# A 31-tap depthwise conv split between TensorE and VectorE: 24 taps stay as matmuls, 7 go to VectorE

## The reference

```
p = x @ w_in     # [B_a | C_a | v_a | val_b | gate_b | g_a | g_b], 1024 columns each
y_a = (B_a * conv3_causal(C_a * v_a)) @ w_out_a
u   = val_b * sigmoid(gate_b)
u   = conv31_causal(u) + conv_b_bias        # depthwise: each channel with its own 31 weights
y_b = silu(LayerNorm(u)) @ w_out_b
x1  = LayerNorm(alpha*x + (sigmoid(g_a)*y_a + sigmoid(g_b)*y_b) @ w_o)
x2  = LayerNorm(alpha*x1 + relu(x1 @ w_up)**2 @ w_down)
```

## Time and profile before

| | us |
|---|---|
| median of 3 runs (lowest, highest) | 2285.79 (2278.91, 2288.07) |
| the profiled execution | 2279.74 |
| its span, slowest core (fastest core) | 2278.2 (2259.3) |
| PE busy | 2159.3, 95% |
| ACT busy | 903.1, 40% |
| DVE busy | 865.2, 38% |
| POOL busy | 625.4, 27% |
| the 2048 conv matmuls, line 424 | 124.0 |

### The profile page before, as it was taken

The page is one execution under the profiler, slowest core; times in us unless marked ns, Lnnn a source line. Parts: engine busy times, 40 slices in busy tenths (PEclk is TensorE's granted clock), DMA queues, the critical chain, the costliest instruction groups (busy, mean ns, idle before and its releaser), DMA issues.

```text
span 2278.2 us, 33259 instructions; the slowest of 8 cores (2259.3 to 2278.2 us)
## 1 busy us (share of the span) xinstructions
PE 2159.3 (95%) x11568; PEld 961.8 (42%) x11568; DVE 865.2 (38%) x1199; ACT 903.1 (40%) x1422; POOL 625.4 (27%) x524
## 2 busy tenths in 40 slices
PE   6997699999997999999999999999999999999896
PEld 2443244443443444444444444444444444444342
DVE  2211154551346233651346034803381237323604
ACT  1111132354324633454335533462346334642562
POOL 1000022330426042421433043404350426030321
PEclk9998899999998999999999999999999999999998
DMA  9999759599886778655566447555665556445452
GB/s 153 140 136 132 187 162 195 188 187 198 207 204 177 200 161 260 198 176 159 190 200 183 156 175 217 180 171 176 188 187 175 177 167 212 140 148 175 139 185 74
DMA packets 107828, 400.69 MB, mean 176 GB/s; under 512 B 13712, under 2 KB 54928, under 8 KB 68752
## 3 DMA queue, kind: packets, MB, share of 16 engines
q1 hardware_dynamic: 84672, 306.21, 42.8%
q0 software_dynamic: 12624, 73.47, 20.7%
q10 hardware_dynamic: 10368, 18.88, 2.6%
HBM read 425.78 MB, written 58.79 MB: 213 GB/s over the span
## 4 chain that ended last, share of the span: by engine, by line
PE 73%; DVE 8%; DMA 7%; SPq 7%; issue 2%; POOL 1%; ACT 1%; DVEq 0%; ACTq 0%; POOLq 0%
PE ps L272 68%; SPq L101 7%; PE ps L424 4%; DVE sgt L295 3%; DMA yblk<-tt 1%; DMA wbf<-wsl 1%; DMA wsl<-wbf 1%; DMA h<-wblk 1%; DVE cvb L282 1%; DMA wsl<-wblk 1%; DMA xft<-xblk 1%; DVE sumS L282 1%; DVE cvh L300 1%; POOL sumQ L282 1%; POOL tt L282 1%
## 5 line engine op out<-in xcount | busy, mean ns | idle before, releaser
L272 PE MATMUL ps<-xbf,wsl 128*128 128x512 bf16 x2624 | 599.1, 381 | 10.8 <-DVE apre L282 6.0
L272 PE MATMUL ps<-bx,wsl 128*128 128x512 bf16 x2560 | 571.0, 380 | 7.6 <-ACT bx L278 7.3
L272 PE MATMUL ps<-h,wsl 128*128 128x512 bf16 x2496 | 545.6, 380 | 9.8 <-DMA wsl<-wblk 9.6
L278 ACT ACTIVATE tA<-ps 128x512 f32<-128x512 f32 x448 | 264.7, 594 | 436.8 <-PE ps L272 403.1
L272 PEld LDWEIGHTS ps<-xbf,wsl 128*128 128x128 bf16 x2624 | 253.2, 98 | 327.3 <-issue 33.5
L272 PEld LDWEIGHTS ps<-bx,wsl 128*128 128x128 bf16 x2560 | 249.2, 98 | 316.4 <-issue 21.7
L272 PEld LDWEIGHTS ps<-h,wsl 128*128 128x128 bf16 x2496 | 244.6, 98 | 307.0 <-issue 14.9
L282 POOL TENSOR_TENSOR tt<-tt,rstd 128x512 f32<-128x512 f32 x178 | 243.5, 1368 | 99.3 <-ACT rstd L278 76.9
L272 PE MATMUL ps<-xbf,h 128*128 128x512 bf16 x1024 | 233.8, 391 | 38.3 <-DVE cvb L295 18.9
L282 POOL TENSOR_TENSOR tt<-res,mu 128x512 f32<-128x512 f32 x112 | 158.4, 1414 | 389.0 <-DMA yblk<-tt 203.5
L282 POOL TENSOR_TENSOR tt<-u,mu 128x512 f32<-128x512 f32 x66 | 90.1, 1366 | 593.7 <-ACT mu L278 539.8
(11 more groups left out here) (66 smaller groups left out, 1150.4 us busy)
## 6 DMA issues: line engine op xcount, KB each, us to landing
wsl<-wbf SPq DMA_DIRECT2D x240, 1024.0 KB, 6.0
rep<-u0d SPq DMA_DIRECT2D x256, 135.0 KB, 3.9
wbf<-wblk POOLq DMA_DIRECT2D x24, 1024.0 KB, 23.7
wsl<-wblk POOLq DMA_DIRECT2D x16, 1024.0 KB, 15.3
yblk<-tt ACTq DMA_DIRECT2D x56, 256.0 KB, 6.0
xbf<-xblk POOLq DMA_DIRECT2D x13, 1024.0 KB, 13.8
xft<-xblk POOLq DMA_DIRECT2D x32, 256.0 KB, 6.5
wbf<-wsl SPq DMA_DIRECT2D x8, 1024.0 KB, 19.5
```

The costliest lines, as they stand in the source:

```text
L272: last = e.matmul(bank_ap, lhsT=l, rhs=r, start=(start and idx == 0), stop=(stop and idx == n - 1))
L278: S.op("act", lambda e: e.activation(out=out, in_=in_, func=func, bias=bias, scale=scale), reads=reads, writes=writes)
```

## The change

KS goes from 8 to 6: TensorE keeps the youngest 24 taps, in 24 matmuls for each conv. The oldest KD = 7 taps go to DVE. A new tile `un` (three buffers, 128 channels x 518 tokens, bf16) is filled from `u0d` by one further DMA in `spread`, without the spreading over partitions. In `conv` ACT writes `u` with the bias as before; then the new `conv_taps` adds tap after tap to `u` with `stt`, in place; only then ACT squares `u` (no longer the bank), `spread` for j + 3 is issued, and the sums are taken. The places move: behind j = 1, 3, 5 of S3 the conv with four taps, with three taps, the Square and the rest behind j = 2, 4, 6; none in S1A(i+1); five in up, behind f = 2, 8, 14, 20, 26. The eight convs of pass 0 keep their places, with all seven taps. The conv weights are halved on chip, as before, the seven in a tile `cwn` of their own.

```diff
-KS = 8
+KS = 6
+KD = KB - 4 * KS
+NUN = 3
+NW = T + KD - 1
...
         def spread(i, j):
...
-            c0 = i * T + 1
+            c0 = i * T + 1 + 32 - 4 * KS
...
+            r = (8 * i + j) % NUN
+            c0 = i * T + HL + 1 - KB
+            S.dma("sp", unsem[r], un[r][:], u0d[j, :, c0:c0 + NW],
+                  reads=[("u0d", i % 2, j)] + ([("u0dh", j)] if i == 0 else []), writes=[("un", r)])
...
-        def conv(i, j, st_):
+        def conv(i, j, st_, whole=True):
...
             act(u[:, j, :], ps[b][:, :], AF.Identity, reads=[("ps", b), "cst"], writes=[("u", j)],
                 bias=pv[:, 0, j:j + 1])
+            rel(b)
+            conv_taps(i, j, st_, 0, KD if whole else KD - 3)
+
+        def conv_taps(i, j, st_, lo, hi):
+            r = (8 * i + j) % NUN
+            for k in range(lo, hi):
+                stt(u[:, j, :], un[r][:, k:k + T], cwn[:, j, k:k + 1], u[:, j, :], ALU.mult, ALU.add,
+                    reads=[("un", r), ("u", j), "cwn"], writes=[("u", j)])
+            if hi < KD:
+                return
             q = rt("sq", 2)
-            act(sq[q][:], ps[b][:, :], AF.Square, reads=[("ps", b), "cst"], writes=[("sq", q)],
-                bias=pv[:, 0, j:j + 1])
-            rel(b)
+            act(sq[q][:], u[:, j, :], AF.Square, reads=[("u", j)], writes=[("sq", q)])
             if j + NREP < 8:
                 spread(i, j + NREP)
...
                 if not last and j in (1, 3, 5):
-                    conv(i + 1, j // 2, stC)
+                    conv(i + 1, j // 2, stC, False)
+                if not last and j in (2, 4, 6):
+                    conv_taps(i + 1, j // 2 - 1, stC, KD - 3, KD)
...
-                    if j in (2, 5):
-                        conv(i + 1, 3 + j // 4, stC)
...
-                if not last and f in (8, 16, 24):
-                    conv(i + 1, 4 + f // 8, stC)
+                if not last and f % 6 == 2 and f < 30:
+                    conv(i + 1, 3 + f // 6, stC)
```

More of the change, by code:

```diff
@@ L132, in build_nc @@
     ident4_d = nc.dram_tensor("ident4", [128, 32], F32, kind="ExternalInput").ap()
+    cwn_d = nc.dram_tensor("cwn", [128, 8, KD], F32, kind="ExternalInput").ap()
     cwa_d = nc.dram_tensor("cwa", [128, 8, KA], F32, kind="ExternalInput").ap()
@@ L164, in build_nc @@
         wsl = [sb(f"wsl{i}", [128, 4096], BF16) for i in range(NS)]
+        cwn = sb("cwn_s", [128, 8, KD], F32)
+        un = [sb(f"un{i}", [128, NW], BF16) for i in range(NUN)]
         cwa = sb("cwa_s", [128, 8, KA], F32)
@@ L186, in build_nc @@
         osem = [S.new_sem(f"o{i}") for i in range(NTT)]
-        csem = [S.new_sem(f"k{i}") for i in range(5)]
+        csem = [S.new_sem(f"k{i}") for i in range(6)]
+        unsem = [S.new_sem(f"un{i}") for i in range(NUN)]
         repsem = [S.new_sem(f"rp{i}") for i in range(NREP)]
@@ L697, in build_nc @@
         S.dma("sp", csem[2], pv[:], pv_d, writes=["cst"])
+        S.dma("sp", csem[5], cwn[:], cwn_d, writes=["cwn"])
+        tsc("dve", cwn[:], cwn[:], 0.5, None, ALU.mult, None, reads=["cwn"], writes=["cwn"])
         for j in range(8):
@@ L901 @@
     wblk = _weight_blocks(f(w_in), f(w_out_a), f(w_out_b), f(w_o), f(w_up), f(w_down))
-    taps = np.zeros((4 * KS, D), np.float32)
-    taps[4 * KS - KB:] = f(conv_b_w)
+    taps = f(conv_b_w)[KB - 4 * KS:]
+    cwn = np.ascontiguousarray(f(conv_b_w)[:KB - 4 * KS].T.reshape(8, 128, KD).transpose(1, 0, 2))
     cwb = np.ascontiguousarray(
@@ L919 @@
             xh = np.ascontiguousarray(x[b, t0 - HL:t0, :].reshape(HL, 8, 128).transpose(2, 1, 0))
-        in_maps.append({"xblk": xb, "xh": xh, "wblk": wblk, "cwb": cwb, "cwa": cwa, "pv": pv,
+        in_maps.append({"xblk": xb, "xh": xh, "wblk": wblk, "cwb": cwb, "cwn": cwn, "cwa": cwa, "pv": pv,
                         "ident4": np.tile(np.eye(32, dtype=np.float32), (4, 1))})
```

## The result

The changed kernel takes **1.0578 times the time of the one before, 95% interval 1.0525 to 1.0631** (both run side by side). Its profiled execution took 2413.4 us against 2279.7: **+133.6 us, where the prediction had +76**. The sign is as forecast; the time lies above the upper end of the range, 2405.

What follows compares the result with a forecast made beforehand. TensorE, busy 95%, bounds the kernel; after the change ACT ends last in up. Passes 1 to 6 +59.4, pass 0 +3.5, start +13: +76 on 2279.7, 2356 profiled, 2362 by the median; range 2322 to 2405.

Steps and rivals of the forecast that it cites:

- The hold of ACT per conv: Up stage: one conv holds ACT 7.34 us, from Identity through seven DVE taps (0.85 us step) to the Square's end.
- The count of the up stage: Up's start to the end of down's first block: 83.6 us instead of 68.0, +15.6, as ACT ends last.
- S1A: Stage losing both its convs: 3.7 us less, plus half of a 1.09 us wait kept, -4.3 us a pass.
- Rivals (1): Up's stall is covered by eight banks, all 29.6 us come off: 2250, by the median 2256; chance 0.04.
- (2): Taps step by 0.60 us, ACT's hold is 5.84: +8, 2288, by the median 2294; chance 0.06.
- (3): Taps step by 1.62 us everywhere, something other than POOL slowing them: +203, 2559, by the median 2565; chance 0.03.
- rival (4): Weights come late behind SP's waits, in each of seven passes: +35, 2391, by the median 2397; chance 0.09.
- The start: F and first S1A: +16 us from DVE's late sums, less 2.8: +13 us, between 8 and 17.
- the -2.8 for shorter convs in F: Six convs stand in F, where TensorE gains 6 x 0.46 = 2.8 us.
- Pass 0: First pass: longer up stage covers down's waits for weights, 10.9 - 1.6 - 4.3 - 1.4 = +3.5 us.
- The step that failed: S3: splitting taps 4 and 3 delays a sigmoid about 3 us, covered by banks; put at nothing.
- 9.9 a pass: Passes 1 to 6: up +15.6, S1A -4.3, S3's three shorter convs -1.4, net +9.9 each, +59.4 together.

Runs made afterwards that it cites:

- both edits: Changed kernel with the convs' Square, spread and sums four f later in up and one j later in S3: 0.9955, again 0.9940, of the kernel before; profiled 2265.8 us.

## Why the prediction was right in sign and short in size

**Right, term by term.** The hold of ACT per conv was put at 7.34 us. The trace has 7.29, from the Identity at 1294.15 to the next operation at 1301.44 (ACT's timeline, and the taps on DVE's):

```profile
1294.15 0.67 ACT L285 ACTIVATE u<-ps,pv_s 128x512 f32<-128x512 f32 x1
1300.90 0.63 ACT L285 ACTIVATE sq<-u 128x512 f32<-128x512 f32 x1 [6.08 <-DVE u L302]
1301.44 0.58 ACT L285 ACTIVATE tA<-ps 128x512 f32<-128x512 f32 x1
```

```profile
1294.92 5.88 DVE L302 SCALAR_TENSOR_TENSOR u<-un,cwn_s,u 128x512 f32<-128x512 bf16 x7 [2.20 <-ACT u L285]
```

Seven taps took 5.88 us for 5.85, and the wait ahead of the Square is 6.08 us for all five convs of this pass. The count of the up stage gave 83.6 us to the end of down's first block, measured 82.9, with the waits where it had them: about 2.3 at f=22 (1.60), 1 to 3 at f=28 (2.49), and the rest at down's first block (5.71). S1A gave back 3.8 us for 4.3. Rivals (1), (2) and (3) are out by the same rows, and rival (4) with them, since waits for wsl<-wbf sum to 3.7 us in the span. (The +203 and +35 of rivals (3) and (4) count from the forecast's 2356, not from the kernel before.)

**The start**: forecast +13 (+16 less 2.8), measured +18.9 (S3(0) at 378.37, before 359.47 in the earlier trace rows). TensorE, start of S3(0), and the fourth block of down in pass 0 (for the next paragraph):

```profile
378.37 3.57 PE L279 MATMUL ps<-apre,wsl 128*128 128x512 bf16 x8 [4.12 <-DVE apre L289]
...
598.10 36.52 PE L279 MATMUL ps<-h,wsl 128*128 128x512 bf16 x157 [5.77 <-DMA wsl<-wblk]
```

S1A to S3 took 304.01 to 378.37, 17.1 us more for a forecast of 16, the sums of j=0 and 1 at 35.7 us for a forecast of 36. What failed is the -2.8 for shorter convs in F: from the first conv to S1A TensorE gained 1.5 us (47.2 us, before 48.7), and the first conv itself, which waits for rep (27.1 us; 12.0 before), started at 256.85, 3.4 us later than before. In the changed kernel it starts between 252.6 and 260.5 us, depending on the core, before between 249.7 and 253.5. I did not test what sets it.

**Pass 0**: forecast +3.5, measured +3.9 (start of down's fourth block 598.10, before 575.31 in the earlier trace rows, less the start's 18.9). That the two agree is luck. The forecast put three blocks of down, 3 x 6.9 us, between the end of the first block and the start of the fourth, where two stand (13.8 us; in the earlier trace rows 160 matmuls, five blocks of eight, are left at its start); by its own terms it should have come to -3.4, and the sum to 69. It also took the waits for weights as covered, which they are not: they are 2.75 and 5.77 us. The wait of 5.77 us stands just where the block too many had been counted, so that the up stage to the fourth block is 9.0 us longer for a forecast of 9.3. S3 to up was 5.1 us shorter for 5.7.

**The step that failed** is a term that was put at nothing: "the split into 4 and 3 taps delays a sigmoid by about 3 us, which the banks cover: nothing, and the taps at 1.62 us beside POOL still fit". Two things are wrong in it. The size: ACT idles ahead of the three Squares of S3 for 5.2, 6.8 and 8.6 us, and the sigmoid behind the third one, whose matmuls had ended at 1213.51, starts at 1221.21, 7.7 us late and not 3. The taps stand in DVE's queue behind the products of their j, which wait for TensorE, and the second and third time they run beside a busy POOL and take 4.1 and 5.1 us in place of 2.5. And the question: I asked whether TensorE's banks cover ACT's delay. They do; TensorE does not wait in this S3, which takes 52.9 us for 54.2 before. But the queue behind the Square held also the y stores, which return POOL's buffers, and the x loads; these ended at the sums of mix, where no bank helps. It cost 8.9 to 10.7 us in each of passes 2 to 6, 47.9 us of the 57.6 that are missing. Another 5.9 are missing at the start.

The sum then reads: start 18.9; pass 0 3.9; passes 1 and 2 together 25.3; passes 3 to 6 together 85.3 (19.7, 22.8, 21.6 and 21.2: the distances between down's first sums of successive passes, 259.7 to 261.5 us, less those of before); the last 0.2 behind them: 133.6 us. The forecast had 9.9 a pass from pass 1 on. In pass 3 the trace gives 14.9 in up, -3.8 in S1A and -0.4 from there to mix (for -1.4: the clock returns only behind down's first sums), 10.7 together, and 9.0 in mix: 19.7.

The waits in up and in mix have the same cause, one that the prediction named for one stage and did not look for in the other.

## What to carry to other kernels

An operation that waits for another engine can cost what everything behind it in its queue costs, DMA issues included. For each, list what stands behind it and who is waiting for that, in every stage where it occurs, not only where the waiting engine is the bound. And before giving up on work moved to an idle engine, move the operation that collects its result: here four f or one j later turned 1.058 into 0.994.

## What the runs showed of the hardware

A DVE operation that takes its running sum from the one before steps by 0.85 us (seven in 5.88), where unchained ones step by 0.60. Those are of another kind (`tensor_tensor`); three unchained ones of the same kind, in mix of the changed kernel, step by 0.60 as well (one operand comes from PSUM there):

```profile
1224.70 1.88 DVE L302 SCALAR_TENSOR_TENSOR res<-xft,ps 128x512 f32<-128x512 f32 x3 [0.70 <-PE ps L279]
```

The recorder puts a semaphore wait ahead of each chained one, for DVE itself, so the 0.85 us is the step with that wait; how much of it the wait makes is not shown. Beside POOL, the same three taps of a conv take twice as long. DVE's timeline of the changed kernel, in S3, once with POOL idle, once with POOL at work from 1212.43 to 1218.72:

```profile
1182.70 2.46 DVE L302 SCALAR_TENSOR_TENSOR u<-un,cwn_s,u 128x512 f32<-128x512 bf16 x3
...
1214.17 5.09 DVE L302 SCALAR_TENSOR_TENSOR u<-un,cwn_s,u 128x512 f32<-128x512 bf16 x3
```

The rule of the Trainium skill, SBUF — State Buffer, section "Who interferes with whom", that a VectorE operation with two inputs in SBUF and a GpSimd one that reads SBUF exclude each other, agrees in that both slow down: a tap takes 1.57 to 1.75 us for 0.75, and the three POOL operations beside the taps 1.53 to 1.71 us for 1.26. One of each in turn for its whole length would be 2.0 us a pair; the trace has 1.7. I cited it for the up stage, where it does no harm; in S3, where it does, I counted the slow taps only against DVE's time and not against ACT's wait.

TensorE's clock is part of each wait's price. The stretches around the wait for h (us, PE, PEld, DVE, ACT, POOL busy, granted clock, DMA share, GB/s):

```profile
1355.00:1364.00 9.00, 5.05 (x23) 2.12 (x22) 4.87 (x7) 4.63 (x9) 0.00 (x0) 0.94 0.43 155
1364.00:1368.00 4.00, 2.19 (x6) 0.85 (x7) 0.00 (x0) 1.57 (x3) 0.00 (x0) 0.50 0.49 209
1368.00:1372.00 4.00, 4.00 (x16) 1.63 (x15) 1.38 (x2) 1.69 (x4) 1.26 (x1) 0.77 0.57 188
```

Behind 5.71 us of waiting six matmuls took 2.72 us at a granted clock of 0.50 (1.2 GHz) where they take 1.3, and the granted clock was 0.50 until 1369 and 1.00 again from 1370 on. Over a whole run the mean is 0.953 in the changed kernel, 0.977 with both edits and 0.980 before.
